# Three product units side by side behind each norm, square sums spread over all partitions, and start-up loads in two parts

## What is computed

```python
def rmsnorm(x, g):
    xf = x.astype(jnp.float32)
    y = xf * lax.rsqrt(jnp.mean(xf * xf, axis=-1, keepdims=True) + EPS)
    return (y * g.astype(jnp.float32)).astype(x.dtype)

def modulated_norm(x, g, shift, scale):
    return rmsnorm(x, g) * (1 + scale[:, None]) + shift[:, None]

def half_ffn(x, mod, g, w_up, w_down):
    h = modulated_norm(x, g, mod[:, 0], mod[:, 1])
    a, b = jnp.split(h @ w_up, 2, axis=-1)
    return x + FFN_RES * mod[:, 2][:, None] * ((jax.nn.silu(a) * b) @ w_down)

def trunk_layer(x, c, lw, token_mix):
    mod = (jax.nn.silu(c) @ w_ada + b_ada).reshape(c.shape[0], N_SUB, 3, D_MODEL)
    x = half_ffn(x, mod[:, 0], g_norm[0], w_ff_up[0], w_ff_down[0])
    h = modulated_norm(x, g_norm[1], mod[:, 1, 0], mod[:, 1, 1])
    ...
    x = half_ffn(x, mod[:, 2], g_norm[2], w_ff_up[1], w_ff_down[1])
```

## Time and profile before

| | |
|---|---|
| median of 3 runs | 3165.66 us (3161.19 to 3166.5) |
| the profiled execution, its own time | 3163.12 us |
| its span in the profile | 3161.5 us |
| PE busy | 3097.9 us (98%) |
| DVE, ACT busy | 1190.1 us (38%), 840.8 us (27%) |
| mean granted TensorE clock | 0.991 |

### The profile page before, as it was taken

How to read it: one execution, slowest core, us unless ns; L and a number is a source line. 1 busy time by engine, 2 the same in 40 slices (tenths; PEclk the granted TensorE clock), 3 DMA queues, 4 the chain that set the end, 5 groups by cost and what they waited for, 6 DMA issues and landing times. The chain is left out here.

```text
span 3161.5 us, 54219 instructions
## 1 busy us (share of the span) xinstructions
PE 3097.9 (98%) x23440; PEld 2765.0 (87%) x23440; DVE 1190.1 (38%) x2091; ACT 840.8 (27%) x1281; POOL 138.5 (4%) x269
## 2 busy tenths in 40 slices
PE   8999999999999999999999999999999999999999
PEld 6999998877777899999999999988776878899999
DVE  4333334344432344333353323442534223533333
ACT  3221224332321123212232212242324212322121
POOL 0000000000411000000000000000003120000000
PEclk9999999999999999999999999999999999999999
DMA  6444442111358432333223444312022682322212
GB/s 237 150 173 158 160 145 84 68 54 37 100 175 268 137 122 101 133 141 116 85 83 136 170 172 150 125 62 94 29 75 65 215 289 91 116 81 87 101 71 79
DMA packets 119047, 390.00 MB, mean 123 GB/s; under 512 B 12828, under 2 KB 63356, under 8 KB 100504
## 3 DMA queue, kind: packets, MB, share of 16 engines
q1 hardware_dynamic: 100608, 338.36, 30.1%
q0 software_dynamic: 14432, 34.09, 3.1%
q10 hardware_dynamic: 3768, 14.08, 1.1%
HBM read 372.79 MB, written 13.69 MB: 122 GB/s over the span
## 5 line engine op out<-in xcount | busy, mean ns | idle before, releaser
L1621 ACT ACTIVATE w_hi<-w 128x1024 fp32r<-128x1024 f32 (+2 forms) x232 | 266.0, 1147 | 1229.4 <-PE g L868 905.0
L868 PE MATMUL g<-h_hi,w_hi 128*128 128x272 f32 x2688 | 561.0, 290 | 8.4 <-ACT area L1631 4.5
L868 PE MATMUL g<-h_hi,w_lo 128*128 128x272 f32 x2688 | 556.6, 288 | 0.0
L868 PE MATMUL g<-h_lo,w_hi 128*128 128x272 f32 x2688 | 553.5, 287 | 0.0
L2200 DVE TENSOR_TENSOR w_lo<-w,w_hi 128x1024 fp32r<-128x1024 f32 (+2 forms) x232 | 309.5, 1336 | 496.0 <-ACT w_hi L1621 493.0
L868 PEld LDWEIGHTS g<-h_hi,w_hi 128*128 128x128 f32 x2688 | 422.0, 189 | 27.2 <-ACT area L1631 16.3
L868 PEld LDWEIGHTS g<-h_lo,w_hi 128*128 128x128 f32 x2688 | 421.0, 188 | 0.0
L868 PEld LDWEIGHTS g<-h_hi,w_lo 128*128 128x128 f32 x2688 | 420.4, 188 | 0.0
L868 PE MATMUL g<-h_hi,w_rest 128*128 128x272 f32 x1280 | 370.2, 289 | 0.0
L868 PE MATMUL g<-acts_hi,w_hi 128*128 128x272 f32 x1408 | 305.7, 291 | 0.1
L868 PE MATMUL g<-acts_hi,w_lo 128*128 128x272 f32 x1408 | 301.2, 288 | 0.0
(11 more groups left out here) (308 smaller groups left out, 4248.9 us busy)
## 6 DMA issues: line engine op xcount, KB each, us to landing
w<-in_w_up SPq DMA_DIRECT2D x43, 2048.0 KB, 7.8
w<-in_w_ada SPq DMA_DIRECT2D x32, 2048.0 KB, 7.9
w<-in_w_in SPq DMA_DIRECT2D x16, 2048.0 KB, 8.1
w<-in_w_down SPq DMA_DIRECT2D x16, 1536.0 KB, 6.9
w<-in_w_gate SPq DMA_DIRECT2D x48, 512.0 KB, 5.6
w<-in_w_down SPq DMA_DIRECT2D x16, 1280.0 KB, 5.7
area<-in_cache_k SPq DMA_DIRECT2D x72, 256.0 KB, 3.9
area<-in_cache_v SPq DMA_DIRECT2D x72, 256.0 KB, 4.5
```

Source lines behind the costliest of these rows:

```text
L868: return pe.matmul(o, a, b, start=start, stop=stop, skip_group_check=True, **kw)
L1621: ac.activation(WH[i % 2][:, 0:n], W[place][:, o:o + n], ACT.Copy).then_inc(s_wh, 1)
```

## The change

Behind norms 1 to 5 three units instead of two are multiplied h block by h block; the third stands in the banks of `Q`. The square sums of a half are made in four groups of 68 columns, one on each 32 partitions, so that root and inverse work on 128 partitions x 68 instead of 64 x 136. The splits of the first three or four weight blocks are made in the last steps of the stage before, and the units split during the second half are four and five. The Silu table is loaded between the sixth and the seventh block of the second half. At the start the loads `WA[1]` to `WA[3]` go out as halves on both queues, and both vectors behind the first blocks are made together. The core of the diff:

```diff
+def first_together(n):
+    return 2 if n == 0 else 3
...
-        SUMS = [TB[64 * h:64 * h + 64, h, 300:300 + QT] for h in range(2)]
+        SUMS = [TB[:, h, 300:300 + QH] for h in range(2)]
@@ SP queue: start, and the release of a layer's first stage @@
-            sp.dma_start(WA[2], d["w_ada"][ADA_ORDER[2][1]]).then_inc(s_first[2], 16)
-            sp.wait_ge(s_first[2], 16)
+            for i in range(1, FIRST_ADA):
+                sp.dma_start(WA[i][:, 0:SLOT // 2], d["w_ada"][ADA_ORDER[i][1]][:, 0:SLOT // 2]).then_inc(s_first[i], 16)
+            sp.wait_ge(s_first[FIRST_ADA - 1], 32)
...
-                        sp.wait_ge(s_unit, units.value() - 2)
+                        sp.wait_ge(s_unit, units.value() - 4 + first_together(3 * what[0] + 2 * what[1]))
@@ PE: norm_sum, spread_roots, last_pair, behind_first_blocks, first_pair @@
-                    for j in (2 * h, 2 * h + 1):
-                        last = mm(TB[32 * j:32 * j + 32, h, 300:300 + QT], ones[:, 0:32], H[:, k, j * QT:(j + 1) * QT],
-                                  k == 0, k == KD - 1)
+                    for j in range(4):
+                        o = h * HALF + j * QH
+                        last = mm(SUMS[h][32 * j:32 * j + 32], ones[:, 0:32], H[:, k, o:o + QH], k == 0, k == KD - 1)
...
-                mm(TB[:, h, 0:HALF], ones[r], RS[r, h * HALF:(h + 1) * HALF], True, True).then_inc(s_rs, 1)
+                mm(TB[:, h, 0:HALF], ones, RS[:, h * HALF:(h + 1) * HALF], True, True).then_inc(s_rs, 1)
...
-                            if (h, r, k) == (1, 0, 3):
+                            if (h, r, k) == (1, 0, 2):
                                 norm_sum(KD - 1, 0, (0,))
-                            if (h, r, k) == (1, 0, 7):
+                            if (h, r, k) == (1, 0, 6):
                                 spread_roots(n, 0)
...
                 if q == 3:
                     vectors(2)
+                    vectors(3)
                 if q == 4:
                     features(2)
                 if q == 5:
-                    vectors(3)
-                if q == 6:
                     features(3)
...
-            def first_pair(n, weights_of, rest):
+            def first_units(n, weights_of, rest):
...
+                def block(r, h, k):
+                    bank = (G[:, 2 * p[r] + h] if r < 2 else Q[:, h])[:, 0:HALF]
+                    last = thirds(bank, weights_of(r, 0, k), weights_of(r, 1, k), k, h, k == 0, k == KD - 1,
+                                  of=(HH, rest))
...
-                    for r in range(2):
...
+                    for r in range(first_together(n)):
+                        block(r, h, k)
-                    if n and q == 1:
+                    if n and q == 2:
                         norm_sum(KD - 1, 0, (1,))
-                    if n and q == 4:
+                    if n and q == 5:
                         spread_roots(n, 1)
@@ ACT: roots, first_norm, norm, ffn, start, mixer @@
-                ac.activation(RS4[r], SUMS[h], ACT.Sqrt, bias=EPSC[r, 2:3], scale=1024.0 / D).then_inc(s_rms, 1)
+                ac.activation(RS4[:, h], SUMS[h], ACT.Sqrt, bias=EPSC[:, 2:3], scale=1024.0 / D).then_inc(s_rms, 1)
...
+                    if q == 4:
                         rows(2)
+                        rows(3)
...
+                    if q in (9, 10):
+                        if q == 9:
+                            ac.wait_ge(s_w[0], LANDED[0])
+                        then()
+                    if q == 13:
+                        silu_table()
...
-                    if q in (10, 12):
-                        then((q - 10) // 2)
+                    if split and q in (10, 12):
+                        split()
+                    if table and q == 13:
+                        table()
...
+                        third = (half, c) == (0, 1) and at[0] > 4
+                        chunk(c, not half == c == 0 and not third, not half == c == 0, Q[:, :, 0:HALF] if third else None)
...
+                        if norm_next and m >= PAIR - 2:
+                            begin, end = ((0, 2), (2, 4 if f == 0 else 3))[m - PAIR + 2]
+                            if f == 0:
+                                hi_part(l, *[("ua", i) for i in range(begin, end)])
+                            else:
+                                first_hi(l + 1, 0, range(begin, end))
...
-            for i in range(1, FIRST_ADA, 2):
-                ac.dma_start(WA[i], d["w_ada"][ADA_ORDER[i][1]]).then_inc(s_first[i], 16)
+            for i in range(1, FIRST_ADA):
+                ac.dma_start(WA[i][:, SLOT // 2:], d["w_ada"][ADA_ORDER[i][1]][:, SLOT // 2:]).then_inc(s_first[i], 16)
...
-                each(4, lambda i, p: ac.activation(halves(YA[:, i, :]), both(p), ACT.Gelu_apprx_tanh,
+                each(4, lambda i, p: ac.activation(halves(YA[:, i, :]), Q[:, :, 0:HALF] if i == 2 else both(p),
+                                                   ACT.Gelu_apprx_tanh,
                                                    bias=ZERO[:, 0:1]), l, {i: [("va", i)] for i in range(4)})
...
-                        first_hi(l, 1)
+                        first_hi(l, 1, range(3))
@@ DVE: inverse_roots, first_norm, norm, ffn, add_to_x @@
-                link(ve.reciprocal(RS4[r], RS4[r]))
+                link(ve.reciprocal(RS4[:, h], RS4[:, h]))
...
-                biased(2)
-                biased(3)
+                    if q == KD - 2:
+                        biased(2)
+                biased(3)
+                low(0, KD - 1)
...
-                weights_ahead(0)
                 add_first(0)
-                weights_ahead(1)
+                weights_ahead(2)
...
+                def weights_ahead(nth):
+                    for i in ((0, 1), (2,), (3,))[nth]:
+                        if f == 0:
+                            lo_part(l, ("ua", i))
+                        elif i < 3:
+                            first_lo(l + 1, 0, i)
...
+                        if half == 1 and norm_follows(l, f) and m >= PAIR - 2:
+                            weights_ahead(m - PAIR + 2)
...
+                    if m == PAIR - 1:
+                        for i in range(3):
+                            first_lo(l, 1, i)
```

More of the change, by code:

```diff
@@ L438, in build @@
         DIAG, o_d = take(2, P)
-        RS4, _ = take(QT, start=o_d)
+        RS4, _ = take(2, QH, start=o_d)
         SMALL, _ = take(36)
@@ L454, in build @@
         FIRST_HI = [over(f"w_hi_a{i}", o, 1024) for i, o in enumerate((o_yb, o_yb + 1024, o_k, o_k + 1024))]
-        UA_HI = EARLY_HI + FIRST_HI[2:4]
+        THIRD_HI = over("w_hi_third", o_f + 6 * T, 1024)
+        UA_HI = EARLY_HI + [over(f"w_hi_ua{i}", o_tv + 5 * 512 + 1024 * i, 1024) for i in range(2)]
         LATER_HI = FIRST_HI[0:2] + [over(f"w_hi_b{i}", o_s + 1024 * i, 1024) for i in range(2)]
@@ L505, in first_weights @@
         def first_weights(l, f, i):
-            hi = (EARLY_HI if l and not f else MIDDLE_HI)[i]
+            hi = THIRD_HI if i == 2 else (EARLY_HI if l and not f else MIDDLE_HI)[i]
             return hi[:, :], WR[AT["ffn", (l, f, 0)] % 2][:, i * UP_BLOCK:(i + 1) * UP_BLOCK]
@@ L732, in release @@
                     splits.n += FFN_UNITS[what[2]]
+                    if what[2] == 0:
+                        together = first_together(3 * what[0] + 2 * what[1])
+                        splits.n -= together
+                        firsts.n += together
+                        sp.wait_ge(s_wf, firsts.value())
                     units.n += FFN_UNITS[what[2]]
@@ L1005, in first_pair @@
                         behind_first_blocks(q)
+                if n:
+                    un.take()
             def split_in(l, job):
@@ L1024, in first_products @@
             def first_products(l, f):
-                w = [first_weights(l, f, r) for r in range(2)]
-                wait(wl, 2)
-                first_pair(3 * l + 2 * f, lambda r, i, k: w[r][i][:, k * P:(k + 1) * P], HL)
+                together = first_together(3 * l + 2 * f)
+                w = [first_weights(l, f, r) for r in range(together)]
+                wait(wf, together)
+                first_units(3 * l + 2 * f, lambda r, i, k: w[r][i][:, k * P:(k + 1) * P], HL)
             def ffn(l, f):
@@ L1047, in ffn @@
                             first_products(l, f)
-                        for u in range(2 if i == 0 else 0, 4):
+                        for u in range(first_together(3 * l + 2 * f) if i == 0 else 0, 4):
                             one(u % 2, KD, HH, HL)
@@ L1565, in first_norm @@
                 rows(1)
-                for q in range(KD + 1):
-                    if q == KD:
-                        rows(3)
+                for q in range(2 * KD):
                     hi_of_h(0, q)
@@ L1571, in first_norm, with norm @@
                         samples_hi(slice(0, 4))
-                    if q == 5:
+                    if q == 4:
                         rows(2)
-                for q in range(KD + 1, 2 * KD):
-                    hi_of_h(0, q)
```

(29 more changed lines are left out.)

58 lines of the change are left out of this document (24 added, 34 removed).

## The result

The changed kernel takes 3140.8 us (median of 4 runs, 3137.9 to 3145.2) beside 3163.4 for the kernel before: a ratio of 0.9929 [0.9912, 0.9946]. Measured once more beside other kernels it took 3143.1, 0.9940 [0.9926, 0.9954].

A forecast was written before the change was run, and what follows sets the result against it. PE, busy 98% of the span, was taken as the bound, so only its idle and slow time could be won: 8.9 + 1.7 + 0.3 + 2.0 + 1.7 = 14.6 us off 3163.1, plus 2.5 for the median: 3151.0, range 3143 to 3160.

The forecast's parts named there:

- Three units: Behind norms 1 to 5: a third unit fills PE's waits up to unit four, 8.9 us won in all.
- Square sums: Sums on all partitions: 1.7 us from the wait ahead of the first spread, 0.3 from shorter half sums.
- The start: Start of the kernel: 2.0 us from loads and order (0.5 to 3.5), plus 1.7 from the clock.
- The order behind the first blocks: In the start: moved splits and table cut the 2.38 idle to about 0.6; table delays two blocks by 1.2.
- The clock: In the start: one of two stretches at 1.2 GHz goes, 1.7 us won, bounds 0 and 3.4.
- The median: Whole kernel: median taken to lie 2.5 us above the profiled execution, so 3148.5 became 3151.0.
- What was forecast to cost nothing: Splits moved into the stage before, and SP releasing a layer's first slot some 4 us later: no cost.
- Short waves have no floor: Rival, square sums: 68-column waves cost as much as 136, whole sums lose 0.24 us, 30 times; 3159.0, chance 0.09.
- DVE does not end the norm: Rival, norms 2, 3 and 5: DVE's splits and product delay unit four some 2.3 us; 3157.9, chance 0.12.
- The table takes its 1.28: Rival, three norms and start: Silu table load costs twice that, PE waits some 1.2 us; 3155.8, chance 0.05.
- The weights are not late: Rival, ahead of norms 1, 3 and 4: late first weights stall PE, ending slower than 3165.7; chance 0.05.
- The change does what it says: Rival of no effect: second half stays bound by DVE, only sums and start win about 4 us; 3161.7, chance 0.09.

The follow-up runs named there:

- the filled waits: Kernel before, with multiplications nobody reads put into PE's waits in the start: 3164.9 us (1.0005), and with counts sized to the waits 3159.4 us (0.9987).
- the faster versions: Changed kernel with second spread one block earlier (3135.6 us); also with Gelu ahead of the split and third unit's last three blocks held back (3136.8 us).

## Why the prediction fell short

**Three units: right.** 8.9 was forecast and 8.95 measured, in each norm within 0.1. The second half begins 11.03 behind S (11.25 forecast) with 0.93 idle (0.9), and the late spread is what it waits for, as the run with the spread early shows. Unit four then waits for DVE's product (0.88; forecast 1.0) or for Gelu (1.60; 1.8). One attribution in it is wrong: in norms 1 and 4 the third unit wins nothing, it costs 0.42. There the 0.85 was forecast for the right kernel and the wrong part of it.

**Square sums: mis-sized, 2.0 for 4.64.** Two terms of this step failed, both ahead of S. The whole sum was put at +0.04 us, 30 times; it is +0.004, 25 times: 1.1 us. The spread was put at nothing ("twice the rows and the same columns"); on 128 rows it begins 0.09 sooner behind the last product and lets PE go on 0.20 sooner, five times: 1.5. The wait ahead of it (0.35), the half sum's 0.10 and the inverse (578 ns; 0.58 forecast) were right. The row of 32-column instructions from which the 0.04 was drawn did not tell enough: the direct measure, the time from a sum to the next product, stands in the trace of before for 136 columns only, and a small loss taken 30 times ate 1.2 of the 2.0 that were sized right.

**The start: mis-sized, 3.7 for 6.05.** The loads in two parts were put at 1.4: the visible wait of 1.86, less 0.4. They give 3.3 in the first profile (35.44 against 32.10) and 1.9 in the second (33.57). The step that failed is to take the visible wait for the whole slack. PE reached that wait late, because in before the first vector ran at the slow clock, 3.25 us where the changed kernel's first profile has 1.90:

```profile
20.96 3.25 PE L868 MATMUL q<-area,cond 128*32 128x512 f32 x16
```

The load's landing at 29.2 to 29.4 was the fixed point. Once the load is early, PE's own chain decides. In the first profile it ran at full speed, 1.86 + 1.35 = 3.2; in the second its first vector took 3.23, and the visible 1.86 is what is won. So of the 2.35 by which the start was sized too small, 1.4 are this execution's luck with the clock. The order behind the first blocks was put at 0.6 and gives 1.2. The clock was put at 1.7, one stretch of two; by the filled waits it is 1.5 behind unit three and next to nothing ahead of it. The size came out right by luck: both stretches of the earlier trace rows went and not one, and most of what they had cost lay ahead of a wait for something else.

**The median: 2.5 added, 4.4 the other way.** The forecast is in effect the sum taken from a median of three executions, 3165.7; later series of the same kernel have 3161.5 to 3163.5. The changed kernel's executions spread over 7 us by the clock in the mixers and single late loads, and its profiled one was the slowest of four. Neither figure says anything about the change; the range had room for the 2.5 only.

**What was forecast to cost nothing.** ACT's wait for the first weights one unit earlier holds up no S. The release by SP comes 0.8 us ahead of unit four (1201.60), 5.7 ahead in before (1208.04): some 4.9 later against the need (some 4 forecast), and the loads behind it are issued where they were (45.6 behind unit four in norm 2, 45.4 before). The -1.8 elsewhere is a balance of single steps of 0.3 to 1.7 us. Two of them: a load of cached keys was late in the first mixer (the wait for in_cache_k above; 1.2 us, in this execution and not in the second), and in the layer behind norm 2 a weight load took longer, so that the split behind it was late. Its landing (KB, us) after and before, and PE after:

```profile
w<-in_w_up SPq DMA_DIRECT2D x1, 2048.0 KB, 9.3
```

```profile
w<-in_w_up SPq DMA_DIRECT2D x1, 2048.0 KB, 7.5
```

```profile
1259.76 0.49 PE L880 MATMUL g<-h_hi,w_hi 128*128 128x272 f32 x2 [1.24 <-DVE w_lo L2220]
```

It cost 1.3 us of lead in this execution and 0.5 in the second profile of the same kernel, where the same load landed 8.4 us behind its issue: the load's length varies, its issue does not.

**The rivals.** Short waves have no floor (0.374). DVE does not end the norm: its splits end 0.42 us before PE gives it the product in norm 3, a margin that the faster versions use up. The table takes its 1.28, and ACT's next instruction stands 1.29 behind its start. Behind norms 2, 3 and 5 no wait of PE follows; in the start one does, 0.87 us ahead of the fifteenth block, whose high part ACT makes behind the table. DVE in norm 3, then PE in the start:

```profile
1622.51 0.72 DVE L2237 TENSOR_TENSOR area<-area,g 128x544 f32<-128x544 f32 x1 [0.42 <-PE q L880]
```

```profile
53.97 0.39 PE L880 MATMUL g<-h_hi,w_hi_middle 128*128 128x272 f32 x1 [0.87 <-DVE h_lo L2080]
```

The weights are not late. The change does what it says.

## What to carry to other kernels

A wait that is seen is what is left after everything else that was slow ahead of it, so when its cause is removed the gain is the distance from the fixed point (here a load that lands at 29.2 us) back along the engine's own chain at the clock that it then gets (3.3 or 1.9 here), not the wait. In this start a stretch at the slow clock cost only where nothing but that engine was late; filling the waits ahead of it showed which part that was. Put the spread of a statistic where its consumer becomes free, not where it is convenient: one block earlier was worth 1.1 us in each norm, some half of what the third unit wins in a feed-forward norm.

## What was not expected of the hardware

PE on 128 rows is done with a spread of 272 columns sooner than on 64: 0.356 us to the next product against 0.653, with the product behind it 0.1 slower. Where nothing holds it up it also begins sooner behind the last product, 0.126 against 0.217.

Half a square sum in 8 short instructions of 68 columns takes 0.256 us, in 4 of 136 columns 0.356.

The slow clock in the start differs between executions of the same kernel, and goes with the wait ahead of the fifth square sum. Of eleven profiled executions of kernels with and without the change five waited 1.94 to 2.44 us there and then ran the first vector at the lower level in part (2.7 to 3.3 us); six waited 0.92 to 1.53 and ran it in 1.90, one of them with the gap filled. The wait ends at 18.8 to 19.0 in all of them; it is long where the first sum began early (15.2 to 15.8, in the other unfilled ones 16.2 to 16.8) and nothing filled the gap. That a full engine takes the stretch away is shown by the fills; what makes the sums begin early, no run shows.

Loads of 2 MB fall into two groups. Of 93 from 60 us on, 55 (before) and 60 (after) land 7.4 to 8.1 us behind their issue, 31 and 26 land 8.2 to 9.1, and seven in each take longer. Which load is in which group is kept between two executions of the changed kernel (88 of 93) far more than between the two kernels (62 of 93). So it goes with the program more than with the execution; what in the program sets it, no run here shows.
